# Index scores in units between the natural products, the sample's index steps between u chunks, transposes in shared banks, sample ties inside the key stage

## What is computed

```python
u, q, k, v, qi, ki, wi, gates = split(rms_norm(x, ln1) @ w_in)
a_pool = pool_mixer(u, ...)                 # windows of 2, 4, 8, 16 tokens, mean minus token, per-group map
s = einsum('bqhd,bld->bqhl', qi, ki) * IDX_DIM ** -0.5          # index scores, 4 heads of 64
score = einsum('bqh,bqhl->bql', wi * IDX_HEADS ** -0.5, relu(s))
idx = top_k(where(k_pos <= q_pos, score, -inf), 256)[1]         # 256 keys for each query
a_attn = softmax(q . k[idx] * HEAD_DIM ** -0.5 + rel_bias) . v[idx]
m = sigmoid(g1) * (a_pool @ w_pool_proj) + sigmoid(g2) * (a_attn @ w_attn_proj)
h = x + m @ w_out
y = rms_norm(h + swiglu(rms_norm(h, ln2)))
```

## Time and profile before

| | us |
|---|---|
| median of 3 runs | 1785.67 |
| lowest, highest | 1774.81, 1785.86 |
| the profiled execution | 1784.01 |
| its span | 1782.2 |
| PE busy | 1672.0 |
| DVE busy | 775.4 |
| ACT busy | 478.9 |
| POOL busy | 447.4 |

### The profile page before, as it was taken

How to read it: one execution, slowest core, us unless ns; L and a number is a source line. 1 busy time by engine, 2 the same in 40 slices (tenths; PEclk the granted TensorE clock), 3 DMA queues, 4 the chain that set the end, 5 groups by cost and what they waited for, 6 DMA issues and landing times.

```text
span 1782.2 us, 25675 instructions
## 1 busy us (share of the span) xinstructions
PE 1672.0 (94%) x10060; PEld 1425.0 (80%) x10060; DVE 775.4 (44%) x1927; ACT 478.9 (27%) x923; POOL 447.4 (25%) x379
## 2 busy tenths in 40 slices
PE   7997799688999998899999999999999999999997
PEld 4544366445569866688889999999999999999996
DVE  2215999997910066511244442323323323323315
ACT  2113211154452255521143322111121121111113
POOL 3000107220524432111112252232232232232220
PEclk9996899899999999999999999999999999999999
DMA  5500511072651000122301231111111111111002
GB/s 174 105 21 24 172 36 37 12 272 88 195 189 48 24 1 1 44 78 82 95 25 36 71 95 48 41 46 43 36 50 44 47 47 47 47 47 47 0 1 107
DMA packets 115842, 116.95 MB, mean 66 GB/s; under 512 B 17438, under 2 KB 104110, under 8 KB 112685
## 3 DMA queue, kind: packets, MB, share of 16 engines
q1 hardware_dynamic: 102471, 73.74, 13.8%
q0 software_dynamic: 5312, 39.33, 6.9%
q10 hardware_dynamic: 7982, 2.83, 0.6%
HBM read 107.66 MB, written 8.45 MB: 65 GB/s over the span
## 4 chain that ended last, share of the span: by engine, by line
PE 55%; DVE 1%; ACT 1%; DMA 0%; issue 0%; DVEq 0%; ACTq 0%
PE banks L108 52%; PE banks L1669 3%; DMA out_dram<-yo 0%; DVE yo L1993 0%; PE banks L1658 0%; ACT XH L1826 0%; DVE rinv L1958 0%; ACT junk L1900 0%; ACT sH L1819 0%; ACT resid L1823 0%; PE banks L1761 0%; PE banks L1707 0%; DVE gated L1913 0%; ACT fst L1902 0%; ACT rinv L1870 0%
## 5 line engine op out<-in xcount | busy, mean ns | idle before, releaser
L108 PE MATMUL banks<-hnH,wH 128*128 128x344 f32 x1056 | 338.7, 321 | 3.8 <-DVE sg L1967 3.8
L108 PE MATMUL banks<-hnH,wL 128*128 128x344 f32 x1056 | 337.4, 320 | 0.0
L1791 POOL TENSOR_TENSOR wL<-w_raw,wH 128x1024 fp32r<-128x1024 f32 (+1 forms) x55 | 155.8, 2849 | 204.2 <-ACT wH L1850 203.8
L108 PEld LDWEIGHTS banks<-hnH,wH 128*128 128x128 f32 x1056 | 198.9, 188 | 4.4 <-issue 4.3
L108 PEld LDWEIGHTS banks<-hnH,wL 128*128 128x128 f32 x1056 | 198.8, 188 | 0.0
L1981 DVE TENSOR_TENSOR resid<-resid,banks 128x344 f32<-128x344 f32 x264 | 134.9, 512 | 107.4 <-PE banks L108 107.3
L1339 DVE TENSOR_SCALAR_CACHE_REDUCE pta<-SC,thr 128x384 uint8<-128x384 f32 (+2 forms) x192 | 176.1, 942 | 4.6 <-POOL SC L835 2.5
L108 PE MATMUL banks<-aH,wH 128*128 128x344 f32 x528 | 169.4, 321 | 1.6 <-DVE resid L1981 1.6
L108 PE MATMUL banks<-aH,wL 128*128 128x344 f32 x528 | 169.7, 321 | 0.0
L108 PE MATMUL banks<-hnL_lo,wH 128*128 128x344 f32 x528 | 169.0, 320 | 0.0
L108 PE MATMUL banks<-aL,wH 128*128 128x344 f32 x528 | 168.5, 319 | 0.0
(11 more groups left out here) (295 smaller groups left out, 2924.7 us busy)
## 6 DMA issues: line engine op xcount, KB each, us to landing
w_raw<-in_w_gate_up_dram SPq DMA_DIRECT2D x44, 512.0 KB, 3.9
w_raw<-in_w_down_dram SPq DMA_DIRECT2D x11, 1024.0 KB, 4.8
big<-in_w_in_dram SPq DMA_DIRECT2D x12, 512.0 KB, 4.0
W<-in_x_prompt_dram SPq DMA_DIRECT2D x8, 512.0 KB, 6.9
slab_raw<-in_w_in_dram SPq DMA_DIRECT2D x8, 512.0 KB, 4.3
x_nat<-in_x_prompt_dram SPq DMA_DIRECT2D x8, 512.0 KB, 4.1
slab_raw<-in_w_out_dram SPq DMA_DIRECT2D x8, 512.0 KB, 4.0
out_dram<-yo SPq DMA_DIRECT2D x8, 512.0 KB, 2.6
```

What stands on the lines that cost most here:

```text
L108: last = nc.tensor.matmul(out, w_cols(w, k), x_cols(x, k), start=(k == 0 and j == 0), stop=(k == nk - 1 and j == 2))
L1791: gp.tensor_tensor(wL[p], w_raw[p], f32(wH[p]), ALU.subtract).then_inc(w_lo, 1)
```

## The change

- The 24 pairs (block, head) of the index scores become 40 units of at most 512 columns (`UNITS`), each in bank 2 or 3. The units of block t - 2 are issued inside `natural(t)`, between its products (4 or 8 units over 16 products); those of block 7 inside the first u chunk. ACT's ReLUs and DVE's additions go with them, before `natural_out(t)` and before `naturalT_out(t - 1)`. POOL's causal selects follow block by block.
- `transpose_natural` writes to banks 0 and 1, which `transpose_x` uses; each waits until DVE has read the other's.
- `kid` and `kidT` move to the memory of `Dp`, `rl` to that of `pta`; POOL gathers the first two `kid` at the start of its part, before the scores.
- u and q chunks rotate over banks 5, 6 and 7 and are straight code. Chunk 0 carries the units of block 7, chunk 1 stands between the sample's query steps, chunk 2 + b between the transposes and the products of sequence b, chunk 10 before the sums, chunk 11 before the last transpose, 12 between the state's and the tail's transposes, 13 to 23 follow.
- The products of the sample's ties stand inside the key stage, at step 6.
- `transpose_max` comes after projection chunk 0 instead of before it, and the other three steps beside the chunks come one chunk later.
- POOL waits for the sample's sums and the natural outputs before it mixes.

The core of the diff:

```diff
+            UNITS = [(i, h, c0, min(512, lens[i] - c0)) for i in range(FIRST_TOPK, NBLK) for h in range(IH) for c0 in range(0, lens[i], 512)]
...
+                def score_unit(n):
+                    i, h, c0, w = UNITS[n]
+                    half = slice(h % 2 * HD, h % 2 * HD + HD)
+                    pe.wait_ge(natT_evac, i + 1)
+                    if n >= 2:
+                        pe.wait_ge(relu_done, n - 1)
+                    mm(ps[:, 2 + n % 2, 0:w], qiT[half, h // 2, tile_cols(i)], kiT[half, c0:c0 + w], start=True, stop=True).then_inc(idx_ready, 1)
...
+                    scored = units_of(t - 2)
+                    for q in range(2 * KD):
+                        k = q % KD
+                        if q < KD:
+                            mm(ps[0:r, 4 + t % 2, 0:NKVC], hT[:, k, tile_cols(t)], w_kv[:, k, :], start=k == 0, stop=k == KD - 1)
...
+                        if scored and q % (2 * KD // len(scored)) == 0:
+                            score_unit(scored[q * len(scored) // (2 * KD)])
...
                     pe.wait_ge(nat_evac, t + 1)
-                    if t:
+                    pe.wait_ge(hT_ready, 2 * min(t + 2, NT - 1) + 2)
+                    if t == NT - 1:
                         pe.wait_ge(natT_evac, t)
...
                     if t + 1 < NT:
+                        if t >= 2:
+                            pe.wait_ge(natT_evac, t - 1)
                         transpose_x(t + 1)
...
+                slab_chunk(0, units_of(NBLK - 1))
+                pe.wait_ge(qid_ready, 1)
                 pe.wait_ge(natT_evac, NT)
...
                     last.then_inc(kid_used, 1)
+                    slab_chunk(2 + b)
                     pe.wait_ge(kidT_evac, b + 1)
...
+                slab_chunk(10)
                 pe.wait_ge(sidx_relu, 1)
...
+                slab_chunk(11)
                 pe.wait_ge(ssp_done, 1)
                 tr(ps[:, 4, 0:P], SP1[:, :], ident[:, :]).then_inc(ssT_ready, 1)
...
+                slab_chunk(12)
+                pe.wait_ge(uq_evac, 12)
...
+                for x in range(13, UQ):
+                    slab_chunk(x)
...
                     if m:
                         key_logits(m - 1)
+                    if m == TIES_AT:
+                        sum_sample_ties()
...
-                transpose_max()
-                beside = {1: transpose_negmax, 3: sum_probs, 5: transpose_sample_probs}
+                beside = {0: transpose_max, 2: transpose_negmax, 4: sum_probs, 6: transpose_sample_probs}
...
                 pool.wait_ge(setup_step, 8)
+                load_kid(0)
+                load_kid(1)
+                for i in range(FIRST_TOPK, NBLK - 1):
+                    causal(i)
...
-                pool.wait_ge(uq_evac, 6 + 12)
+                pool.wait_ge(uq_evac, 12)
                 pool.wait_ge(stT_evac, 1)
-                pool.wait_ge(sidx_used, NB)
+                pool.wait_ge(ssc_ready, 1)
+                for b in range(2):
+                    pool.wait_ge(nat_out[b], 48 * len(range(b, NT, 2)))
...
+                    for n in units_of(t - 2):
+                        score_out(n)
                     if t >= 1:
                         naturalT_out(t - 1)
```

More of the change, by code:

```diff
@@ L181, in decoder_layer @@
             ap_w = place("ap_w", 2 * D, [2, 4, P], F32, SC_at)
+            kid = Dp.rearrange("p g n -> p (g n)")[:, 0:2048].rearrange("p (b n) -> p b n", b=2)
+            kidT = Dp.rearrange("p g n -> p (g n)")[:, 2048:4096].rearrange("p (b n) -> p b n", b=2)
             kT = sb("kT", [P, 2, TOK])
@@ L563, in _ @@
-                pe.wait_ge(sm_step, SM["ties"])
-                pe.wait_ge(upto_made, 1)
-                mm(ps[:, 6, 0:P + 2], same16[:, :, :].rearrange("p b r -> p (b r)"), seq[:, :], start=True, stop=True)
-                mm(ps[:, 6, 256:256 + P + 1], upto16[:, :], seq[:, 0:P + 1], start=True, stop=True).then_inc(sm_made, 1)
-                pe.wait_ge(zq_ready, 1)
-                pe.wait_ge(uq_evac, 6 + 24)
+                pe.wait_ge(st_in, 16)
+                for g in range(NG):
+                    last = tr(ps[:, 0, g * 120:(g + 1) * 120], st_nat[:, g * P:(g + 1) * P], ident[0:120, 0:120])
@@ new lines, in _, with sum_sample_ties @@
+                last.then_inc(stT_ready, 1)
+                slab_chunk(12)
+                pe.wait_ge(uq_evac, 12)
+                for g in range(NG):
+                    last = tr(ps[0:POOLBUF + NB, 1, g * P:(g + 1) * P], U[:, g, 16 + SEQ - POOLBUF:16 + TOK], ident[:, :])
+                last.then_inc(uT_ready, 1)
+                for x in range(13, UQ):
+                    slab_chunk(x)
+                def sum_sample_ties():
+                    pe.wait_ge(sm_step, SM["ties"])
+                    pe.wait_ge(upto_made, 1)
+                    mm(ps[:, 6, 0:P + 2], same16[:, :, :].rearrange("p b r -> p (b r)"), seq[:, :], start=True, stop=True)
+                    mm(ps[:, 6, 256:256 + P + 1], upto16[:, :], seq[:, 0:P + 1], start=True, stop=True).then_inc(sm_made, 1)
@@ L843, in _ @@
+                causal(NBLK - 1)
+                for b in range(2, NB):
+                    pool.wait_ge(kid_used, b - 1)
+                    load_kid(b)
                 pool.wait_ge(setup_step, 3)
@@ L1025, in _ @@
                   ACT.Copy).then_inc(qid_ready, 1)
+                for n in units_of(NBLK - 1):
+                    relu_unit(n)
+                uq_out(0)
                 act.wait_ge(zi_ready, 2)
@@ L1033, in _ @@
                 A(wsel[:, :], ps[0:64, 1, 0:NB], ACT.Copy).then_inc(zi_copied, 1)
-                act.wait_ge(natT_ready, NT)
-                for b in range(2):
-                    act.wait_ge(nat_out[b], 48 * len(range(b, NT, 2)))
+                uq_out(1)
                 for b in range(NB):
@@ L1071, in _ @@
                 act.dma_start(new_pool_sample[0, :, POOLBUF - 1, :], upo[POOLBUF:POOLBUF + NB, :]).then_inc(pool_out, 16)
[L1072 to L1078 removed]
+                for x in range(13, UQ):
+                    uq_out(x)
+                act.wait_ge(uq_evac, UQ)
                 for g in range(2):
```

197 lines of the change are left out of this document (87 added, 110 removed).

## The result

| | before | after |
|---|---|---|
| median | 1784.65 us (4 runs, 1774.81 to 1785.86) | 1834.54 us (4 runs, 1819.98 to 1835.65) |
| span of the profiled execution | 1782.2 us | 1831.7 us |
| first search starts | 173.03 us | 199.39 us |
| second search starts | 228.50 us | 280.13 us |
| TensorE (PE) idle ahead of the ties' product | 16.0 us | 38.0 us |

The changed kernel is slower: ratio 1.0288, 95% interval 1.0251 to 1.0325, or some 50 us. The forecast was 1806.5 with 1817 as its upper end. So the direction and the mechanism held, and the size did not: 28 us are missing.

The account below looks back on a forecast made before the run. DVE's selection chain was taken to bound the kernel up to the maximum at about 430 us, then PE. Sum: 1784.0 + 24.9 (later second search) - 2.45 (one projection chunk at quick pace) = 1806.5 us; range 1788 to 1817.

Parts of the forecast that it names:

- the second entry: Sample's scores `ss_ready`, needed by the second search: eleven u chunks put ahead in PE's queue start it 24.9 us later.
- changes of shape in the array: Score units between full-size products on PE: 6 us at most for 40 units, nothing at least; 1 us taken.
- the chunks 0 and 1: First u chunks on PE: 4.64 us each, chunk 0 with block 7's scores (6.9 us) ending at 173.8.
- What bounds the kernel: Up to 430 us DVE's selection chain, ending in the maximum `smx`; from there PE, which has 22.6 us of slack before.
- The second search itself: DVE's search over blocks 4, 5 and the sample: 120.0 us as before, 17.6 of them from POOL's mixing.
- Rival C: POOL's mixing falls into DVE's wait, saving 17.6 us (1789), or score steps overlap more; together chance 0.13.
- The shared banks: Natural stage: `transpose_x` waits for DVE's copies, some 1.15 us on PE for each of six tiles, 7 us.
- ACT, held by its DMA issues: Natural stage: block 2's units queue behind ACT, held 8.95 us at tile 6; 1.5 us taken, range 0 to 6.
- Where PE would stand: PE idles some 35 us ahead of the ties and about 29 us for `smx`; q chunks end at 310.2.
- rival D: PE's own work sets the pace, not DVE's chain; 22.6 us earlier q chunks and 22.6 us waits count: 1739; chance 0.09.
- Rival B: Delays ahead of the first entry add up (ACT 4.5 us, shape switches 5 more): up to 9.5 us, to 1816; chance 0.08.
- the first entry: Last index score, which starts DVE's first search: forecast at 175.3 against 173.03 before, so the chain is freed no earlier.

## Why the prediction was wrong in its size

The mechanism of the second entry was right. What failed are two prices ahead of it: "changes of shape in the array", put at 1 us and measured at 14.8, and the chunks 0 and 1, costed at full clock with no term for a fall, which cost 14.5 us more.

Right:
- What bounds the kernel: the chain of DVE up to the maximum, then PE. Each experiment that moved the maximum moved the end, until the masks took over.
- The second entry. The wait ahead of the second search was 25.4 us (forecast 22.6), in the same place, and eleven chunks moved behind it gave 25.3 us.
- The second search itself. Its length did not change, and neither did what POOL's mixing costs it: 1784.0 + 51.6 - 2.45 reproduces the measured time to 2 us. Rival C, the mixing outside the search, did not occur: it began at 280.56, right behind DVE's start.
- The shared banks: six waits of 1.05 us (line 462, for DVE's copies), forecast 1.15. ACT, held by its DMA issues for 7.45 us at 77.09, delayed PE in no wait that the trace shows, so the 1.5 us put there were too much.
- Where PE would stand: 38.0 us ahead of the ties (forecast 35), 29.1 ahead of the maximum (29). But the q chunks ended at 335.8, not 310.2, because they too stood behind the late stage.
- The sign: rival D, in which PE sets the pace, needed the sample's scores by 210; they came at 280.

Wrong:
- **"Changes of shape in the array": 1 us taken, 6 us as the upper end.** Measured: in the natural stage 24 units at 0.39 us, 9.4, and 8 in the ninth tile at 0.29, 2.3, and 8 x 0.39 = 3.1 us in chunk 0, 14.8 us in all. The row it rested on was mis-read. The product ahead of that one-column product fills 64 columns, not 128, and the 0.15 us from its start to that of the next instruction do hold changes, but the length of a tiny product says little about what a change does to full-length products on both sides of it. The price has to be read as the distance between starts in a repeating pattern; the earlier trace rows had no such pattern with products of 128 rows on both sides. The rule that stood beside it, in the Trainium skill (TensorEngine Tiling (Array Packing), Key Properties: switching the tiling mode drains the engine), spoke against the change and was right in direction. It has no number; the runs here give 0.38 to 0.39 us for the pair of switches between fp32 products of 344 or 512 columns (0.58 and 0.86 us).
- **No term for the granted clock.** Chunk 0 was costed at 11.5 us by rows at 1.00 and took 26.0; chunk 1 at 4.64 and took 7.75. Of these 17.6 us 3.1 are changes of shape and 14.5 are the low clock (11.4 and 3.1, by the experiment with the wide ninth tile). The kernel before ran in the low level too, in other places (about 134 to 158 us and 171.7 to 182 us), and the prediction does not mention it. The range did not hold this term.
- **Rival B** had this form (more delay ahead of the first entry moves everything) and was bounded at 9.5 us. The first search started 24.1 us later than forecast. Its two named causes were not enough without the clock.

The sum of what was missed is 9.6 (natural stage) + 14.5 (clock) + 3.1 (shapes in chunk 0) = 27.2 us ahead of the second search, against 280.1 - 253.4 = 26.7 measured there. In the 9.6 the shapes are 11.7 instead of 1; ACT's 1.5 and 0.7 of the banks' 7 were not needed, and some 1.1 us have no cause shown.

What stays open is why the clock fell. With the changed kernel's half-height units it fell behind the natural products of the ninth tile, which fill 8 columns. It did not fall when these were made over 128 columns, nor when the units had full height, nor when the same half-height units stood in pairs, with the narrow products left as they were. The traces agree on this: all four of kernels with single half-height units and the narrow tile show the fall (at 173.8 to 174.1 us), and none of the eight with one of the three edits has it in chunk 0. In the kernel before, too, the clock fell (at 134.3 us) among the first half-height scores behind the narrow tile. So neither the narrow products nor the units alone are the cause; each of three edits sufficed to remove the fall. No run separates more than that. Nor is it shown that the fall comes in every execution: one of the four of the changed kernel took 1819.98 us, 15 us less than the others, at a mean granted clock of 0.973 against 0.964 to 0.967. This is about what the low clock costs, but there is no trace of that execution. The Trainium skill (TensorE: Matmul & The Clock Gate, What's actually happening) ties the clock to how busy the engine has been; here the engine was without a gap from 171.9 us on, and in the variants without a fall the same wait of 1.14 us stands ahead of chunk 0 and no gap in it, so its busy time in the rows does not tell the two cases apart.

## What to carry to other kernels

Find the one hand-over that sets the end (here the maximum of the sample) and ask of every part of a change what it does to that; work put ahead of its inputs costs its full price there, however well it fills gaps on the busy engine, and two waits in series must be removed together. Some 25 us of the changed kernel, as much as from moving eleven chunks, came from one number, the round after which a value that has long been final is taken. Small products of half height belong in pairs from opposite halves, not one by one between full products.

## What the runs showed of the hardware that I had not expected

- A change from 128-row to 64-row fp32 products and back costs 0.38 to 0.39 us per place at the 2.4 GHz level (1.83 against 1.44 us, 3.26 against 2.88 us), whether one or two products stand there.
- Between products that fill 8 columns, a 128-column product costs 0.29 us per place over its columns, and the same with 64 rows as with 128 (2.24 and 2.25 us against 1.95). A full-height product between wide ones costs nothing extra (1.44 us for 856 columns at 1.68 ns), so width counts as well as height.
- Two products in opposite halves of the rows overlap fully when they are adjacent: 1.06 us for two of 512 columns, 1.91 us for two in the same half. With a full product between them nothing is left of that. The Trainium skill (TensorEngine Tiling (Array Packing), Key Properties) says that tiles work independently of each other; the pairs from opposite halves agree.
- The granted clock fell to 0.50 and stayed there for some 30 us in which PE was busy without a gap, and stayed at 1.00 over the same stretch with the same units in pairs: 26.0 against 13.3 us for chunk 0.
